# Out-projection squares in a PSUM bank, and the tail of chunk 0 ordered ahead of chunk 1

## The chip, the cores and the metric

One NeuronCore of a Trainium2 chip runs the whole kernel. The metric is device time in microseconds (us) from the start of the program to its end. Matmuls run on TensorE (PE), elementwise work on VectorE (DVE), ScalarE (ACT) and GpSimd (POOL), and SyncE (SP) issues the DMAs. SBUF is the on-chip memory of 128 partitions; PSUM has 8 banks of 512 float32 per partition, into which TensorE accumulates.

## What is computed

One inference step of one decoder layer: 1024 prompt tokens and 8 x 4 sample tokens, 1056 together, with 1024 channels. Everything is float32. The part around the change is `_finish`:

```python
mix = jnp.concatenate([attn_o.reshape(b, t, D_ATTN).astype(x.dtype), conv_o], axis=-1)
h = x + mix @ w_out
hn = rms_norm(h, norm_ffn_g)
return h + (jax.nn.silu(hn @ w_gate) * (hn @ w_up)) @ w_down

def rms_norm(x, g):
    xf = x.astype(jnp.float32)
    y = xf * lax.rsqrt(jnp.mean(xf * xf, axis=-1, keepdims=True) + RMS_EPS)
    return (y * g.astype(jnp.float32)).astype(x.dtype)
```

`w_out` is 1024 x 1024; the feed-forward width is 2816. Ahead of this stand a first norm, the input projection, three-branch attention and a short convolution; a final norm follows.

## The kernel before

Channels lie on partitions, tokens on the free axis. The 1056 tokens are cut into three chunks c = 0, 1, 2 of 352 columns, and 1024 channels into 8 tiles k or n of 128. A product is made in three passes from high and low parts (`three_pass`): both operands are split into a rounded part (fp32r) and the rest. One job is one 128 x 352 output tile over 8 input tiles, so 24 matmuls. The weights come as units of 128 x 1024; GpSimd splits each unit into `w_hi` and `w_lo` (a cast, L396, and a subtraction, L398) in a ring of three slots, after a wait for the jobs that last read the slot. The units of the out-projection are OUT0 to OUT0+7, those of the feed-forward begin with FFN0; FFN0+3 has a slot of its own.

Every engine runs its own program in the written order and waits on semaphores. In the out-projection:

- TensorE runs 24 jobs j in the order `OUT_ORDER`: tiles 0 and 1 of every chunk, tiles 2 to 4 chunk by chunk within a tile, then tiles 5 to 7 of chunk 0 (j = 15 to 17), of chunk 1 (18 to 20) and of chunk 2 (21 to 23). Job j goes to bank j % 6.
- VectorE adds each product to the residual (`add_product`, L1503: "evacuation", counts `h_done`). ScalarE squares the result into one of six SBUF buffers (`square`, L1059, counts `h_sq`). VectorE adds the squares of a chunk up in `ssum` (`add_squares`, L1513, counts `h_ss`), always one job behind the evacuation.
- When a chunk is complete, TensorE multiplies `ssum` with a matrix of ones (`sum_of_squares`, L854), which adds over the partitions: behind job 18 for chunk 0, behind job 22 for chunk 1 (`SUMS_BEHIND = [18, 22]`), and behind the first gate tile for chunk 2.
- Then, per chunk: VectorE divides by 1024 and adds epsilon (`mean_square`, L1186), ScalarE takes the root (`take_root`, L936), VectorE the reciprocal (L1192). For each of 8 tiles VectorE multiplies residual, gain and reciprocal (L1193, counts `y_done`), ScalarE copies that to the high part (`normal_hi`, L931, counts `hi_done`), VectorE subtracts for the low part (L1201, counts `lo_done`).
- The first feed-forward group follows in the order `FIRST_JOBS`: for each chunk c the tiles (0, c), (1, c) of the gate and (2, c), (3, c) of the up-projection (n, c). The gate tile (n, c) gets a silu on ScalarE (L1065) before the up tile (n + 2, c) may start, since they use the same bank. Tile (0, c) waits for all eight low parts of chunk c.

ScalarE needs a table load before a root and before a silu when the table in place is the other one; squares and copies work with either.

Of the kernel before, what the change touches and what calls it, by code (L numbers as in the profile page):

```python
# [28 lines left out]
P = 128  # L29
# [6 lines left out]
NC = 3  # L36
# [37 lines left out]
def build(nc, xT, w, gains, taps, conv_state, state_k, state_v, yT, kT, v_out, conv_tail):  # L74
    with ExitStack() as ctx:
# [305 lines left out]
        def _(pool):  # L381
# [104 lines left out]
            for u in range(OUT0 + 3, FFN0 + 16):  # L486
                straight(u)
                hidden_low(0, u)
# [21 lines left out]
        def _(pe):  # L510
# [11 lines left out]
            def tile_job(bank, c, slot):  # L522
                for k in range(KT):
                    mm = three_pass(ps[:, bank, 0:CH], slot, k, slice(P * k, P * k + P),
                                    act_hi[:, k, cols(c)], act_lo[:, k, cols(c)], k == 0, k == KT - 1)
                mm.then_inc(job_done, 1)
# [183 lines left out]
            def out_job(j):  # L710

                n, c = OUT_ORDER[j]
                unit_ready(OUT0 + n)
                if j < 2:
                    pe.wait_ge(biased, 2 * STEPS)
                if j >= 6:
                    pe.wait_ge(h_done, j - 5)
                if j == 2:
                    pe.wait_ge(act_copied, copied_through(STEPS, 0))
                    pe.wait_ge(dve_copied, copied_through(STEPS - 1, 1))  # L720
                for i, k in enumerate((4, 5, 6, 7, 0, 1, 2, 3)):
# [3 lines left out]
                    mm = three_pass(ps[:, j % 6, 0:CH], (OUT0 + n) % RING, k, slice(P * k, P * k + P),  # L725
                                    hi[:, k % 4, cols(c)], lo[:, k % 4, cols(c)], i == 0, i == KT - 1)
                mm.then_inc(job_done, 1)
# [134 lines left out]
            def gate_up(it, g, first=False):  # L862
                if first:
                    for i, (n, c) in enumerate(FIRST_JOBS):
                        if n == 0:
                            pe.wait_ge(lo_done, KT * (c + 1))
                        if n >= 2:
                            pe.wait_ge(silu_done, FIRST_GATES.index((n - 2, c)) + 1)
                        unit_ready(FFN0 + n)
                        tile_job(3 * (n % 2) + c, c, None if n == 3 else (FFN0 + n) % RING)  # L870
                        if i == 0:
                            sum_of_squares(2)
                    return
# [55 lines left out]
        def _(act):  # L929
# [124 lines left out]
            def square(which, j):  # L1054
                n, c = H_ORDERS[which][j]
                act.wait_ge(h_done, NC * KT * which + j + 1)
                if j >= 6:
                    act.wait_ge((h_ss, last_ss)[which], j - 5)
                act.activation(sq6[j % 6], res[:, n, cols(c)], ACT.Square).then_inc(h_sq, 1)  # L1059
# [68 lines left out]
        def _(dve):  # L1128
# [59 lines left out]
            def normal(which, c, k, dst):  # L1188

                if k == 0:  # L1190
                    dve.wait_ge(root, NC * which + c + 1)
                    chain(dve.reciprocal(rstd[:, cols(c)], rstd[:, cols(c)]))  # L1192
                dve.scalar_tensor_tensor(dst, res[:, k, cols(c)], g_sb[:, which, k:k + 1], rstd[:, cols(c)],  # L1193
                                         ALU.mult, ALU.mult).then_inc(y_done, 1)

            def norm(which, c):
# [7 lines left out]
                for k in range(KT):  # L1204
# [3 lines left out]
                    normal(which, c, k, norm_slot(i))  # L1208
                    if k >= 1:
                        low(i - 1)  # L1210
                low(KT * c + KT - 1)
# [284 lines left out]
            def add_product(which, j):  # L1496
# [5 lines left out]
                bank = j % 6 if which == 0 else last_bank(j)  # L1502
# [3 lines left out]
            def add_squares(j):  # L1506
                n, c = OUT_ORDER[j]
                dve.wait_ge(h_sq, j + 1)
                if n == 0:
                    dve.tensor_copy(ssum[:, cols(c)], sq6[j % 6]).then_inc(h_ss, 1)  # L1510
# [12 lines left out]
            add_squares(NC * KT - 1)  # L1523
            norm(1, 1)
            mean_square(1, 2)
            norm(1, 2)
# [106 lines left out]
BIAS_BEHIND = [6, 7, 11, 12, 19, 20]  # L1633
SUMS_BEHIND = [18, 22]
# [6 lines left out]
def last_bank(i):  # L1641

    return 3 + i % LAST_RING
# [170 lines left out]
```

## Time and profile before

| | us |
|---|---|
| median of 3 runs | 1327.34 (1326.81 to 1327.90) |
| profiled execution, whole time | 1328.08 |
| its span | 1326.3 |
| TensorE busy | 1305.3, 98% of the span |
| VectorE busy | 477.5, 36% |
| ScalarE busy | 239.5, 18% |
| GpSimd busy | 502.1, 38% |

The span is the time between the first and the last recorded instruction. The out-projection lies from about 450 to 552 us of it; the changed part, the last six jobs and the norm between the out-projection and the first feed-forward group, from about 523 to 582 us. Lines such as L1513 are lines of the kernel before. A matmul's recorded length (0.32 us) is longer than the distance to the next, since matmuls overlap in the array.

### The profile page before, as it was taken

The page shows a single profiled execution, that of the slowest core. Times are in us where ns is not written, and L with a number is a line of the kernel's source. Part 1 is how long each engine was busy: PE and PEld are TensorE (multiplying, and loading weights), DVE is VectorE, ACT ScalarE, POOL GpSimd, SP SyncE. Part 2 cuts the span into 40 slices and gives each one's busy share as a digit, 9 for nine tenths or more (in the row PEclk, how much of TensorE's full clock was granted, in tenths as well). Part 3 has the DMA queues.
Part 4 walks back from the last instruction along what each step waited for, and adds up shares of the span by engine and source line. Part 5 has one row for each costly group of instructions (what it writes and reads, how often), then busy time and mean ns, then how long its engine had stood idle before and what let it go on. Part 6 is the DMA issues. An engine that isn't in the chain of part 4 may idle for free.

```text
span 1326.3 us, 20841 instructions
## 1 busy us (share of the span) xinstructions
PE 1305.3 (98%) x8512; PEld 1226.0 (92%) x8512; DVE 477.5 (36%) x886; ACT 239.5 (18%) x506; POOL 502.1 (38%) x475
## 2 busy tenths in 40 slices
PE   7999999999999999999999999999999999999997
PEld 7999987989666799899999999999999999999997
DVE  7844222444665333850313121221213130303046
ACT  6000110000777411331000000101010101010113
POOL 4432142222654232415343343434343333444335
PEclk9999999999999999999999999999999999999999
DMA  5534566252120221202111111111111111111103
GB/s 196 215 123 174 178 238 223 77 193 80 51 98 30 101 79 32 65 1 76 36 49 48 48 48 48 48 48 48 36 44 48 48 48 48 43 53 33 56 9 133
DMA packets 38084, 107.84 MB, mean 81 GB/s; under 512 B 4016, under 2 KB 16496, under 8 KB 36208
## 3 DMA queue, kind: packets, MB, share of 16 engines
q1 hardware_dynamic: 38000, 106.60, 23.4%
q8 instruction: 67, 1.10, 0.4%
q14 instruction: 17, 0.14, 0.0%
HBM read 95.73 MB, written 10.85 MB: 80 GB/s over the span
## 4 chain that ended last, share of the span: by engine, by line
PE 91%; DVE 4%; ACT 1%; issue 1%; DMA 1%; POOL 1%; SPq 0%; DVEq 0%; POOLq 0%
PE ps L518 20%; PE ps L519 19%; PE ps L520 19%; PE ps L907 6%; PE ps L909 6%; PE ps L908 6%; PE ps L660 3%; PE ps L705 2%; PE ps L684 2%; PE ps L637 1%; PE ps L638 1%; PE ps L639 1%; PE ps L609 1%; PE ps L581 1%; DVE out L1193 1%
## 5 line engine op out<-in xcount | busy, mean ns | idle before, releaser
L518 PE MATMUL ps<-act_hi,w_hi 128*128 128x352 f32 x1608 | 523.1, 325 | 8.6 <-DVE act_lo L1216 8.3
L519 PE MATMUL ps<-act_lo,w_hi 128*128 128x352 f32 x1608 | 516.5, 321 | 0.0
L520 PE MATMUL ps<-act_hi,w_lo 128*128 128x352 f32 x1608 | 516.2, 321 | 0.0
L518 PEld LDWEIGHTS ps<-act_hi,w_hi 128*128 128x128 f32 x1608 | 302.6, 188 | 23.0 <-issue 22.1
L519 PEld LDWEIGHTS ps<-act_lo,w_hi 128*128 128x128 f32 x1608 | 303.1, 188 | 0.2
L520 PEld LDWEIGHTS ps<-act_hi,w_lo 128*128 128x128 f32 x1608 | 302.2, 188 | 0.0
L394 POOL TENSOR_TENSOR gate_cell<-ones 128x1 f32<-128x1 f32 x92 | 18.0, 196 | 677.0 <-PE ps L520 462.6
L398 POOL TENSOR_TENSOR w_lo<-w_stage,w_hi 128x1024 fp32r<-128x1024 f32 x93 | 228.7, 2459 | 7.5
L1534 DVE TENSOR_TENSOR work<-ps,work 128x352 f32<-128x352 f32 x66 | 34.4, 524 | 443.6 <-PE ps L520 443.6
L1544 DVE TENSOR_TENSOR resid<-ps,resid 128x352 f32<-128x352 f32 x240 | 126.0, 525 | 102.7 <-PE ps L909 102.7
L907 PE MATMUL ps<-pair_hi,w_hi 128*128 128x352 f32 x504 | 162.8, 323 | 0.0
L908 PE MATMUL ps<-pair_lo,w_hi 128*128 128x352 f32 x504 | 162.3, 322 | 0.0
L909 PE MATMUL ps<-pair_hi,w_lo 128*128 128x352 f32 x504 | 162.2, 322 | 0.0
L396 POOL CAST w_hi<-w_stage 128x1024 fp32r<-128x1024 f32 x93 | 96.9, 1042 | 13.6 <-DVE work L1224 13.6
L1094 ACT ACTIVATE work<-ps 128x352 f32<-128x352 f32 x60 | 27.9, 464 | 401.4 <-PE ps L520 401.4
L909 PEld LDWEIGHTS ps<-pair_hi,w_lo 128*128 128x128 f32 x504 | 94.9, 188 | 0.0
L908 PEld LDWEIGHTS ps<-pair_lo,w_hi 128*128 128x128 f32 x504 | 94.8, 188 | 0.0
L907 PEld LDWEIGHTS ps<-pair_hi,w_hi 128*128 128x128 f32 x504 | 94.7, 188 | 0.0
L931 ACT ACTIVATE pair_hi<-work 128x352 fp32r<-128x352 f32 (+1 forms) x70 | 36.9, 531 | 286.5 <-DVE work L1534 211.2
L450 POOL TENSOR_SCALAR q_blk<-ident,row_rec 128x128 f32<-128x128 f32 x64 | 43.4, 690 | 71.9 <-DVE row_rec L1408 60.5
L482 POOL TENSOR_TENSOR pair_lo<-work,pair_hi 128x352 fp32r<-128x352 f32 x66 | 60.6, 946 | 0.0
L1503 DVE TENSOR_TENSOR resid<-ps,resid 128x352 f32<-128x352 f32 x48 | 25.0, 523 | 56.7 <-PE ps L520 48.0
(228 smaller groups left out, 1328.6 us busy)
## 6 DMA issues: line engine op xcount, KB each, us to landing
w_stage<-in_w SPq DMA_DIRECT2D x97, 512.0 KB, 3.5
resid<-in_state_k SPq DMA_DIRECT2D x8, 1792.0 KB, 8.0
v_buf<-in_state_v SPq DMA_DIRECT2D x14, 1024.0 KB, 5.4
resid<-in_xT SPq DMA_DIRECT2D x16, 528.0 KB, 7.0
out_yT<-resid SPq DMA_DIRECT2D x24, 176.0 KB, 1.8
q_d<-out SPq DMA_DIRECT2D x12, 176.0 KB, 5.0
out_kT<-out SPq DMA_DIRECT2D x12, 176.0 KB, 1.8
out_v<-out SPq DMA_DIRECT2D x16, 128.0 KB, 2.0
```

The costliest lines, as they stand in the source:

```text
L396: pool.tensor_copy(hi, w_stage[:, stage, :]).then_inc(w_split, 1)
L398: pool.tensor_tensor(lo, w_stage[:, stage, :], f32(hi), ALU.subtract).then_inc(w_split, 1)
L450: pool.tensor_scalar(recip[t % 4][h], ident[:, :], row_rec[:, x:x + 1], None, ALU.mult).then_inc(spread, 1)
L482: pool.tensor_tensor(pair_lo[:, 2 * (g % 2) + f, cols(c)], silu[:, f, cols(c)], f32(pair_hi[:, 2 * (g % 2) + f, cols(c)]), ALU.subtract).t ...
L518: pe.matmul(out, hi, rhs_hi, start=first, stop=False)
L519: pe.matmul(out, hi, rhs_lo, start=False, stop=False)
L520: return pe.matmul(out, lo, rhs_hi, start=False, stop=last)
L660: mm = pe.matmul(ps[:, 2 * h + half, 0:width], st_q[g % 2][r, P * i:P * i + P], st_k[g % 2][r, 512 * x:512 * x + width], start=True, stop= ...
L907: pe.matmul(out, hi, x_hi, start=(f == 0), stop=False)
L908: pe.matmul(out, hi, x_lo, start=False, stop=False)
L909: mm = pe.matmul(out, lo, x_hi, start=False, stop=(f == 1))
L1544: dve.tensor_tensor(res[:, n, cols(c)], ps[:, 6 + i % 2, 0:CH], res[:, n, cols(c)], ALU.add).then_inc(added, 1)
```

## The change

The squares no longer go to six SBUF buffers but to one PSUM bank, number 5 (`OUT_BANKS = 5`); the jobs get five banks instead of six. `add_squares(j)` stands right behind `add_product(j)`. The end is ordered by hand: VectorE does evacuations 19 to 22 and the additions of squares 19 to 21 between the tiles of chunk 0's norm, then the mean of chunk 1, addition 22, the reciprocal of chunk 1, evacuation and addition 23, and only then the norm of chunk 1 and that of chunk 2. ScalarE follows that order; the silus of the first group stand elsewhere. The first tile of a chunk waits for each low part as it comes to it, and GpSimd starts unit FFN0+1 only when chunk 0's low parts are done. The function `norm` is now `inverse_root` and `normals(c, ks)`, with the same instructions in them.

```diff
@@ gpsimd
             for u in range(OUT0 + 3, FFN0 + 16):
+                if u == FFN0 + 1:
+                    pool.wait_ge(lo_done, KT)
                 straight(u)
@@ tensor
-            def tile_job(bank, c, slot):
+            def tile_job(bank, c, slot, lows=None):
                 for k in range(KT):
+                    if lows is not None:
+                        pe.wait_ge(lo_done, lows + k + 1)
...
-                if j >= 6:
-                    pe.wait_ge(h_done, j - 5)
+                if j >= OUT_BANKS:
+                    pe.wait_ge(h_done, j - OUT_BANKS + 1)
...
-                        if n == 0:
-                            pe.wait_ge(lo_done, KT * (c + 1))
...
-                        tile_job(3 * (n % 2) + c, c, None if n == 3 else (FFN0 + n) % RING)
+                        tile_job(3 * (n % 2) + c, c, None if n == 3 else (FFN0 + n) % RING, KT * c if n == 0 else None)
@@ scalar
-                if j >= 6:
-                    act.wait_ge((h_ss, last_ss)[which], j - 5)
-                act.activation(sq6[j % 6], res[:, n, cols(c)], ACT.Square).then_inc(h_sq, 1)
+                if which == 0 and j >= 1:
+                    act.wait_ge(h_ss, j)
...
+                act.activation(sq6[j % 6] if which else ps[:, OUT_BANKS, 0:CH], res[:, n, cols(c)], ACT.Square
+                               ).then_inc(h_sq, 1)
...
-            for j in range(NC * KT):
+            for j in range(SUMS_BEHIND[0] + 1):
                 square(0, j)
-                if j in SUMS_BEHIND:
-                    take_root(1, SUMS_BEHIND.index(j))
-                if j == SUMS_BEHIND[0]:
-                    normal_hi(0)
-            next(first_silus)
+            take_root(1, 0)
+            normal_hi(0, range(0, 2))
+            square(0, 19)
+            normal_hi(0, range(2, 5))
+            square(0, 20)
+            normal_hi(0, range(5, 6))
+            square(0, 21)
+            normal_hi(0, range(6, 8))
+            take_root(1, 1)
+            square(0, 22)
+            square(0, 23)
             normal_hi(1, range(0, 2))
             next(first_silus)
-            normal_hi(1, range(2, 8))
+            normal_hi(1, range(2, 4))
+            next(first_silus)
+            normal_hi(1, range(4, 8))
             take_root(1, 2)
-            normal_hi(2, range(0, 3))
-            next(first_silus)
-            normal_hi(2, range(3, 6))
-            next(first_silus)
-            normal_hi(2, range(6, 8))
+            normal_hi(2, range(0, 8))
@@ vector
-                    dve.tensor_tensor(ssum[:, cols(c)], ssum[:, cols(c)], sq6[j % 6], ALU.add).then_inc(h_ss, 1)
+                    dve.tensor_tensor(ssum[:, cols(c)], ps[:, OUT_BANKS, 0:CH], ssum[:, cols(c)], ALU.add).then_inc(h_ss, 1)
 
-            for j in range(NC * KT):
+            for j in range(SUMS_BEHIND[0] + 1):
                 add_product(0, j)
-                if j >= 1:
-                    add_squares(j - 1)
-                if j in SUMS_BEHIND:
-                    mean_square(1, SUMS_BEHIND.index(j))
-                if j == SUMS_BEHIND[0]:
-                    norm(1, 0)
-            add_squares(NC * KT - 1)
-            norm(1, 1)
+                add_squares(j)
+            mean_square(1, 0)
+            inverse_root(0)
+            normals(0, range(0, 2))
+            add_product(0, 19)
+            normals(0, range(2, 3))
+            add_squares(19)
+            normals(0, range(3, 5))
+            add_product(0, 20)
+            normals(0, range(5, 6))
+            add_squares(20)
+            add_product(0, 21)
+            normals(0, range(6, 7))
+            add_squares(21)
+            normals(0, range(7, 8))
+            add_product(0, 22)
+            mean_square(1, 1)
+            add_squares(22)
+            inverse_root(1)
+            add_product(0, 23)
+            add_squares(23)
+            normals(1, range(0, 8))
             mean_square(1, 2)
-            norm(1, 2)
+            inverse_root(2)
+            normals(2, range(0, 8))
```

How the rows stand on the engines, at three places. First VectorE behind the mean of chunk 0, before (L1503 evacuation, L1513 addition of squares, L1186 mean, L1193 and L1201 the norm's multiply and subtraction):

```order
L1503 TENSOR_TENSOR resid<-ps,resid 128x352
L1513 TENSOR_TENSOR work<-work 128x352
L1186 TENSOR_SCALAR work<-ps 128x352
L1192 RECIPROCAL work<-work 128x352
L1193 SCALAR_TENSOR_TENSOR out<-resid,g_sb,work 128x352 x2
L1201 TENSOR_TENSOR act_lo<-out,act_hi 128x352
L1193 SCALAR_TENSOR_TENSOR out<-resid,g_sb,work 128x352
L1201 TENSOR_TENSOR act_lo<-out,act_hi 128x352
```

and in the changed kernel, where the line numbers are L1514, L1524, L1198, L1203, L1217 and L1210:

```order
L1514 TENSOR_TENSOR resid<-ps,resid 128x352
L1524 TENSOR_TENSOR work<-ps,work 128x352
L1198 TENSOR_SCALAR work<-ps 128x352
L1203 RECIPROCAL work<-work 128x352
L1217 SCALAR_TENSOR_TENSOR out<-resid,g_sb,work 128x352 x2
L1210 TENSOR_TENSOR act_lo<-out,act_hi 128x352
L1514 TENSOR_TENSOR resid<-ps,resid 128x352
L1217 SCALAR_TENSOR_TENSOR out<-resid,g_sb,work 128x352
L1210 TENSOR_TENSOR act_lo<-out,act_hi 128x352
L1524 TENSOR_TENSOR work<-ps,work 128x352
```

The additions read `ps`, and evacuation 19 and addition 19 moved from behind chunk 0's norm to between its tiles. Second, VectorE between the norms of chunks 0 and 1, before:

```order
L1201 TENSOR_TENSOR act_lo<-out,act_hi 128x352 x2
L1503 TENSOR_TENSOR resid<-ps,resid 128x352
L1513 TENSOR_TENSOR work<-work 128x352
L1186 TENSOR_SCALAR work<-ps 128x352
L1503 TENSOR_TENSOR resid<-ps,resid 128x352
L1513 TENSOR_TENSOR work<-work 128x352 x2
L1192 RECIPROCAL work<-work 128x352
```

(the pair L1503, L1513 stands there four times) and in the changed kernel:

```order
L1210 TENSOR_TENSOR act_lo<-out,act_hi 128x352 x2
L1514 TENSOR_TENSOR resid<-ps,resid 128x352
L1198 TENSOR_SCALAR work<-ps 128x352
L1524 TENSOR_TENSOR work<-ps,work 128x352
L1203 RECIPROCAL work<-work 128x352
L1514 TENSOR_TENSOR resid<-ps,resid 128x352
L1524 TENSOR_TENSOR work<-ps,work 128x352
L1217 SCALAR_TENSOR_TENSOR out<-resid,g_sb,work 128x352 x2
```

Only evacuations 22 and 23 are left there, and the reciprocal of chunk 1 moved ahead of the last of them. Third, ScalarE from the first silu of the feed-forward on (L1065 silu, L931 high parts, L936 root), before:

```order
L1065 ACT_TABLE_LOAD
L1065 ACTIVATE work<-ps 128x352
L931 ACTIVATE act_hi<-out 128x352 x2
L1065 ACTIVATE work<-ps 128x352
L931 ACTIVATE act_hi<-out 128x352 x6
L936 ACT_TABLE_LOAD
L936 ACTIVATE work<-work 128x352
L931 ACTIVATE act_hi<-out 128x352 x3
L1065 ACT_TABLE_LOAD
L1065 ACTIVATE work<-ps 128x352
L931 ACTIVATE act_hi<-out 128x352 x3
L1065 ACTIVATE work<-ps 128x352
```

and in the changed kernel (L1073, L933, L938):

```order
L933 ACTIVATE act_hi<-out 128x352 x2
L1073 ACT_TABLE_LOAD
L1073 ACTIVATE work<-ps 128x352
L933 ACTIVATE act_hi<-out 128x352 x2
L1073 ACTIVATE work<-ps 128x352
L933 ACTIVATE act_hi<-out 128x352 x4
L938 ACT_TABLE_LOAD
L938 ACTIVATE work<-work 128x352
L933 ACTIVATE act_hi<-out 128x352 x8
L1073 ACT_TABLE_LOAD
L1073 ACTIVATE work<-ps 128x352 x4
```

The first silu moved behind the first two high parts of chunk 1, and the third, that of gate tile (0, 1), from behind three high parts of chunk 2 to behind all eight.

## Rows read from the trace of the kernel before

**Rows 1.** The page: the span, and each engine's busy time, share and instructions.
```profile
span 1326.3 us, 20841 instructions
PE 1305.3 (98%) x8512; PEld 1226.0 (92%) x8512; DVE 477.5 (36%) x886; ACT 239.5 (18%) x506; POOL 502.1 (38%) x475
```

**Rows 2.** TensorE's waits from 525 to 580 us: in total, times, longest.
```profile
PE ps L854 <- DVE work L1513: 3.9, 3, 2.3
PE ps L518 <- ACT work L1065: 0.3, 1, 0.3
```

**Rows 3.** Timeline, TensorE: start, length, line, operation, [idle before <-releaser].
```profile
526.68 0.32 PE L520 MATMUL ps<-act_hi,w_lo 128*128 128x352 f32 x1
528.05 0.86 PE L854 MATMUL ps<-work,ones 128*128 128x352 f32 x2 [1.05 <-DVE work L1513]
528.91 0.32 PE L519 MATMUL ps<-pair_lo,w_hi 128*128 128x352 f32 x1
...
546.46 0.86 PE L854 MATMUL ps<-work,ones 128*128 128x352 f32 x2 [2.29 <-DVE work L1513]
549.25 0.50 PE L520 MATMUL ps<-pair_hi,w_lo 128*128 128x352 f32 x1
549.55 0.50 PE L518 MATMUL ps<-pair_hi,w_hi 128*128 128x352 f32 x1
...
577.29 0.43 PE L518 MATMUL ps<-act_hi,w_hi 128*128 128x352 f32 x1 [0.26 <-ACT work L1065]
```

**Rows 4.** Windows of TensorE: length, busy, granted clock, DMA share, GB/s.
```profile
544.00:548.00 4.00, 1.71 (x8) 0.93 0.37 131
548.00:552.00 4.00, 4.00 (x18) 0.64 0.42 135
```

**Rows 5.** Timeline, VectorE: two evacuations, one job apart.
```profile
523.22 0.53 DVE L1503 TENSOR_TENSOR resid<-ps,resid 128x352 f32<-128x352 f32 x1 [2.86 <-PE ps L520]
...
527.04 0.53 DVE L1503 TENSOR_TENSOR resid<-ps,resid 128x352 f32<-128x352 f32 x1 [2.86 <-PE ps L520]
```

**Rows 6.** Timeline, VectorE: additions of squares (L1513), norm (L1193), evacuations, reciprocal.
```profile
527.48 0.52 DVE L1513 TENSOR_TENSOR work<-work 128x352 f32<-128x352 f32 x1
532.42 1.08 DVE L1193 SCALAR_TENSOR_TENSOR out<-resid,g_sb,work 128x352 f32<-128x352 f32 x2
...
541.00 0.52 DVE L1503 TENSOR_TENSOR resid<-ps,resid 128x352 f32<-128x352 f32 x1
542.29 0.51 DVE L1503 TENSOR_TENSOR resid<-ps,resid 128x352 f32<-128x352 f32 x1
542.72 2.28 DVE L1513 TENSOR_TENSOR work<-work 128x352 f32<-128x352 f32 x1
...
553.19 3.86 DVE L1513 TENSOR_TENSOR work<-work 128x352 f32<-128x352 f32 x2
556.97 2.34 DVE L1192 RECIPROCAL work<-work 128x352 f32<-128x352 f32 x1
559.34 1.97 DVE L1193 SCALAR_TENSOR_TENSOR out<-resid,g_sb,work 128x352 f32<-128x352 f32 x2
```

**Rows 7.** Timeline, GpSimd: weight splits.
```profile
540.50 0.19 POOL L394 TENSOR_TENSOR gate_cell<-ones 128x1 f32<-128x1 f32 x1 [24.80 <-PE ps L520]
542.06 2.55 POOL L398 TENSOR_TENSOR w_lo<-w_stage,w_hi 128x1024 fp32r<-128x1024 f32 x1
...
552.99 1.04 POOL L396 CAST w_hi<-w_stage 128x1024 fp32r<-128x1024 f32 x1
558.02 2.40 POOL L398 TENSOR_TENSOR pt_lo<-w_stage,pt_hi 128x1024 fp32r<-128x1024 f32 x1
```

**Rows 8.** Timeline, ScalarE: a square, then a table load and silu.
```profile
527.60 0.50 ACT L1059 ACTIVATE work<-resid 128x352 f32<-128x352 f32 x1 [3.32 <-DVE resid L1503]
...
575.48 1.28 ACT L1065 ACT_TABLE_LOAD   x1
576.78 0.46 ACT L1065 ACTIVATE work<-ps 128x352 f32<-128x352 f32 x1
```

More of the change, by code:

```diff
@@ L724, in out_job @@
                         pe.wait_ge(mix_lo, STEPS // 2 - 2 + c)
-                    mm = three_pass(ps[:, j % 6, 0:CH], (OUT0 + n) % RING, k, slice(P * k, P * k + P),
+                    mm = three_pass(ps[:, j % OUT_BANKS, 0:CH], (OUT0 + n) % RING, k, slice(P * k, P * k + P),
                                     hi[:, k % 4, cols(c)], lo[:, k % 4, cols(c)], i == 0, i == KT - 1)
@@ L1056, in square @@
                 act.wait_ge(h_done, NC * KT * which + j + 1)
-                if j >= 6:
-                    act.wait_ge((h_ss, last_ss)[which], j - 5)
-                act.activation(sq6[j % 6], res[:, n, cols(c)], ACT.Square).then_inc(h_sq, 1)
+                if which == 0 and j >= 1:
+                    act.wait_ge(h_ss, j)
+                if which == 0 and j == 0:
+                    act.wait_ge(act_copied, copied_through(STEPS, 0))
+                    act.wait_ge(dve_copied, copied_through(STEPS - 1, 1))
+                if which == 1 and j >= 6:
+                    act.wait_ge(last_ss, j - 5)
+                act.activation(sq6[j % 6] if which else ps[:, OUT_BANKS, 0:CH], res[:, n, cols(c)], ACT.Square
+                               ).then_inc(h_sq, 1)
             def first_silu():
@@ L1186, in mean_square, with inverse_root, normals @@
                 dve.tensor_scalar((rstd if which else r_in)[:, cols(c)], ps[:, bank, 0:CH], 1.0 / D, EPS, ALU.mult, ALU.add).then_inc(mean_sq, 1)
[L1188 to L1196, printed above, removed]
+            def inverse_root(c):
+                dve.wait_ge(root, NC + c + 1)
+                chain(dve.reciprocal(rstd[:, cols(c)], rstd[:, cols(c)]))
+            def normals(c, ks):
                 def low(i):
@@ L1202, in low @@
                                       ALU.subtract).then_inc(lo_done, 1)
-                for k in range(KT):
+                for k in ks:
                     i = KT * c + k
@@ L1207, in norm @@
                         dve.wait_ge(lo_done, i - 1)
-                    normal(which, c, k, norm_slot(i))
+                    dve.scalar_tensor_tensor(norm_slot(i), res[:, k, cols(c)], g_sb[:, 1, k:k + 1], rstd[:, cols(c)],
+                                             ALU.mult, ALU.mult).then_inc(y_done, 1)
                     if k >= 1:
                         low(i - 1)
-                low(KT * c + KT - 1)
+                    if k == KT - 1:
+                        low(i)
             def raw_low(k):
@@ L1501, in add_product @@
                     dve.wait_ge(x2_in[n], 16)
-                bank = j % 6 if which == 0 else last_bank(j)
+                bank = j % OUT_BANKS if which == 0 else last_bank(j)
                 dve.tensor_tensor(res[:, n, cols(c)], ps[:, bank, 0:CH], res[:, n, cols(c)],
@@ L1509, in add_squares @@
                 if n == 0:
-                    dve.tensor_copy(ssum[:, cols(c)], sq6[j % 6]).then_inc(h_ss, 1)
+                    dve.tensor_copy(ssum[:, cols(c)], ps[:, OUT_BANKS, 0:CH]).then_inc(h_ss, 1)
                 else:
                     dve.wait_ge(h_ss, OUT_ORDER.index((n - 1, c)) + 1)
-                    dve.tensor_tensor(ssum[:, cols(c)], ssum[:, cols(c)], sq6[j % 6], ALU.add).then_inc(h_ss, 1)
-            for j in range(NC * KT):
+                    dve.tensor_tensor(ssum[:, cols(c)], ps[:, OUT_BANKS, 0:CH], ssum[:, cols(c)], ALU.add).then_inc(h_ss, 1)
+            for j in range(SUMS_BEHIND[0] + 1):
                 add_product(0, j)
-                if j >= 1:
-                    add_squares(j - 1)
-                if j in SUMS_BEHIND:
-                    mean_square(1, SUMS_BEHIND.index(j))
-                if j == SUMS_BEHIND[0]:
-                    norm(1, 0)
-            add_squares(NC * KT - 1)
-            norm(1, 1)
+                add_squares(j)
[20 more added lines that the diff above has]
+            normals(1, range(0, 8))
             mean_square(1, 2)
-            norm(1, 2)
+            inverse_root(2)
+            normals(2, range(0, 8))
             def hidden_of(it, g, first=False):
@@ L1633 @@
 BIAS_BEHIND = [6, 7, 11, 12, 19, 20]
+OUT_BANKS = 5
 SUMS_BEHIND = [18, 22]
```

## Prediction

> **What bounds the kernel now.** I read the page first: TensorE is busy 98% of the span [rows 1], so the time is TensorE's work plus the few gaps in it, and a change on the other engines can only touch gaps. The list of waits for the stretch 525 to 580 us shows all the gaps that this part has [rows 2]: TensorE waits three times at the ones-matmul of L854 (`sum_of_squares`), 3.9 us together, and once, 0.3 us, for a silu. The timeline of TensorE places them [rows 3]: 1.05 us before the sum of chunk 0 (528.05), 2.29 us before that of chunk 1 (546.46), so 0.55 us of the 3.9 before that of chunk 2, and 0.26 us before the third gate-and-up tile of chunk 1 (577.29), which needs the silu of (0, 1). Behind the second gap the granted clock falls: the two windows of [rows 4] lack 0.07 x 4 + 0.36 x 4 = 1.72 us of clock, that is 3.44 us at 1.2 GHz in place of 2.4. A matmul is then issued every 0.29 us (549.25 to 549.55 in [rows 3]) and not every 0.159 (24 of them in 3.82 us, the distance of two evacuations in [rows 5]). So 3.44 us give back only 3.44 x 0.159 / 0.293 = 1.87: 1.57 us are lost. Gaps and clock together are 4.15 + 1.57 = 5.7 us, the most that the stretch holds.
>
> Why are the sums late? VectorE's rows tell it [rows 6]. An addition of squares (L1513, two operands in SBUF) takes 0.52 us alone (527.48), but 2.28 us at 542.72, and the two at 553.19 take 3.86. GpSimd was in a weight split each time: its subtraction of 542.06 ends at 544.61, and the addition ends 0.4 us later, at 545.00 [rows 7]. The multiplies of L1193 (also two in SBUF) show it at 559.34: 1.97 us for two that take 1.08 at 532.42, while GpSimd's subtraction ran from 558.02 to 560.42 [rows 7]. Evacuations (L1503, PSUM and SBUF) and the reciprocal (one operand) are not stretched: 0.51 us at 542.29 and 2.34 us at 556.97, beside the same subtractions. So VectorE's instructions with two SBUF operands and GpSimd's exclude each other, for a whole instruction, and others run on.
>
> **The change, part by part.** *Additions read PSUM.* 21 of the 24 additions and 3 copies change their source. Nearest row: an evacuation, 0.53 us, also PSUM and SBUF. Most lie in VectorE's idle time between jobs, so they cost nothing; if a square written to PSUM took 0.7 us instead of its 0.50 [rows 8], product, square and addition would still take 1.8 of the 3.82 us that a job lasts. The five banks in place of six ask for an evacuation one job earlier, which is four jobs old: nothing. With one bank for the squares, a square waits for the addition before it, and the high parts wait behind it on ScalarE; in the new order that addition always stands ahead of the evacuation that the square needs, so this wait is never the last.
>
> *Sum of chunk 0.* Job 17's tile is evacuated at 523.22; its square and addition are now done by 523.22 + 0.53 + 0.50 + 0.52 and some 0.1 of signals, 524.9, before job 18 ends at 527.0. Gap 1 goes, 1.05 us, and with the pipeline's refill 1.21 (528.05 less 526.84).
>
> *The interleaved tail, VectorE.* I walk its new order. Evacuation 18 at 527.04, square, addition, mean: 529.1; the root stands behind its table load as now (square to 528.1, load 1.28, root 0.50), and the reciprocal runs from 529.9 to 532.2. Chunk 0's normals: eight multiplies and eight subtractions last from 532.42 to the evacuation at 541.00, 8.6 us. Three evacuations and three additions at 0.44 apart are pushed in: 2.6, of which some 0.5 fills waits for ScalarE. GpSimd begins the split of unit FFN0 at 539.3, when job 21 ends (540.50 less the 1.21): the seventh multiply meets its cast (+0.4) and the sixth subtraction its subtraction of 2.4 (+2.2). Chunk 0 ends at 532.2 + 8.6 + 2.1 + 2.7 = 545.6. The addition of square 20 lies ahead of that collision, near 539.5, so the sum of chunk 1 is ready when TensorE arrives: 526.84 + 0.70 for a sum + 4 x 3.82 = 542.8. **Gap 2 and the fall of the clock behind it go.** Job 23 ends near 547.5. (The new wait of a first tile for each low part only loosens one that [rows 2] do not show.)
>
> Then evacuation 22, mean, root, square and addition: 548.0; the second reciprocal 2.35: 550.3; evacuation 23, square, addition (0.53 + 0.50 + 0.52 and signals): 551.9. TensorE wants the last sum after the first gate tile, at 542.8 + 0.70 + 3.82 + 3.82 = 551.15, so **gap 3 is about 0.85, not 0.55.**
>
> *GpSimd's new wait.* Unit FFN0+1 waits for chunk 0's eighth low part, 545.6 (TensorE releases it at 543.0). Queued behind it are units +1, +2, +3, each 0.13 + 1.04 + 0.15 + 2.4 = 3.7 us [rows 7] and some holds by VectorE: they run on end to 557.3. TensorE needs unit +1 at 552.7, +2 at 556.5; they are done at 549.5 and 553.2. So the wait costs TensorE nothing, but the splits now cover the start of chunk 1's normals: the first multiply at 551.86 is held 1.2 us, the second 0.9, the first subtraction 2.1 (it waits for the subtraction that ends at 557.3). Now only 0.9 is lost there.
>
> *The silus.* Chunk 1's normals: 551.9 + 8.6 + 4.2 = 564.7; mean 565.2, root behind its table load, reciprocal 565.9 to 568.3; the last multiply of chunk 2 ends at 568.3 + 7.6 = 575.9 and the last high part (0.50) at 576.4. Only then does ScalarE reach the table load of 1.28 us and the silu of 0.46 [rows 8]: 578.1. Before, that silu stood between the third and the fourth high part of chunk 2 and was done at 577.24 (576.78 + 0.46). TensorE wants it sooner than before: last sum at 552.0 (+0.70), gate tile (1, 0) to 556.5; a wait of 0.8 for the first silu, which now stands behind two high parts and a table load (557.26); four tiles of 3.82: 572.6. So **a new wait of about 5.5 us** stands before tile (2, 1), which starts at 578.1 where it now starts at 577.3: **0.85 us later**, and all that the first two gaps gave is spent there.
>
> *The clock at the new wait.* [rows 4] show a fall behind 2.29 us of waiting, and none behind 1.05 (the matmul at 528.91 has its usual 0.32 us, [rows 3]). Behind 5.5 us I take one fall of the same price, 1.57 us; below it is 0 (as behind 1.05), above it twice that, 3.1, since the wait is 2.4 times the 2.29. After 578 everything on TensorE follows in the same order with no gap from this part, so the shift stays to the end.
>
> The Trainium skill ("ScalarE: Activation LUTs", What ACT_TABLE_LOAD costs) counts a drain of about 1.38 us with each switch, some 2.66 us in all. Here the silu starts 1.30 us after its load begins, so the row decides; by the page the wait would be 1.4 us longer and the time 1331.2.
>
> **Sum.** 0.85 + 1.57 = 2.4 us on the profiled execution's 1328.08 us (span 1326.3 and 1.8 around it). That execution lies 0.74 above the median, inside what one fall of the clock is worth; I move the median by the same 2.4: 1327.34 + 2.4 = **1329.8 us**. Can be told from no change: about 0.2%, 2.7 us.
>
> **Rivals.** (1) *The forecast*: gaps 1 and 2 traded for the silu wait; 1328.4 to 1331.3. It straddles the bound: 56%, of which 31 below +0.2% and 25 above. (2) *The holds are lighter.* The chain of VectorE has 6.9 us of holds in it (0.4, 2.2, 1.2, 0.9, 2.1), each a matter of which engine asks first. With half of them the wait is near 2 us and the tile starts at 574.7; without a fall of the clock that is 1327.3 - 2.6 = 1324.7 (with one 1326.3), and without any holds up to 5.6 us are won, 1321.7. For it: the splits need not meet those instructions. Against: chunk 1's normals run for 8.6 us and three splits in a row for 11.7. 20%, 18 of them below -0.2%. (3) *The wait as forecast, but no clock lost*: 1327.34 + 0.85 = 1328.2; 10%. (4) *Slower, by the clock*: after the long wait the clock comes back only after twice the 3.44 us; 3.1 + 0.85 = 3.95, 1331.3 or more. It decides for slower once the clock loses over 1.8 us, that is over 4 us at the lower level behind 578. Speaks for it: a wait over twice as long; against: the one fall seen came back at once. 14%.
>
> **How the numbers follow.** Faster is case 2's 18%. Same: 31 + 10 + 2 = 43%. Slower: 25 + 14 = 39%. The low end is case 2 with six tenths of the holds gone (4.2 us, the tile at 573.9 and so 3.4 earlier than now), 1324.0; the high end case 4 with a little more, 1331.8. That leaves some 2 in 10 out.
>
> **What would show it.** In the changed profile: no wait before the first two sums; no addition of squares over 0.6 us; a wait of 0.5 to 1 us at the last sum and at (2, 0); GpSimd's splits of three units end to end from about 546 to 557; ScalarE's silu of (0, 1) behind all 24 high parts at about 577.6; TensorE idle 5 to 6 us before it, and a granted clock under 1 behind that. The prediction is wrong if chunk 2's last high part is done before 574, if (2, 1) starts before 576, or if the clock does not fall, or for longer than 4 us.

## The result, and the profile after

| | median us | range | runs |
|---|---|---|---|
| before | 1327.26 | 1326.56 to 1328.63 | 10 |
| changed | 1330.52 | 1329.84 to 1330.83 | 10 |

The ratio is 1.0021, with a 95% interval of 1.0013 to 1.0029: 0.2% slower, 3.3 us between the medians. The forecast was 1329.8. The interval does not hold 1, so the slowdown is real, if small. The profiled execution of the changed kernel took 1329.98 us, its span is 1328.2.

TensorE's waits from 515 to 590 us (in total, times, longest), which answer to [rows 2]. The three waits for a sum, 3.9 us, are one of 0.6, and the wait for a silu of 0.3 us is two, 5.5 together:

```profile
PE ps L520 <- ACT work L1073: 5.5, 2, 5.1
PE ps L858 <- DVE work L1524: 0.6, 1, 0.6
```

TensorE's timeline in the same profile, for [rows 3]. The sums of chunks 0 and 1 have no wait left. TensorE still waits at the last sum (551.92), for the first silu (556.99) and for the silu of (0, 1) (577.86); behind 577.86 a matmul is issued every 0.29 us, until 581.4:

```profile
527.13 0.75 PE L858 MATMUL ps<-work,ones 128*128 128x352 f32 x2
...
551.92 0.86 PE L858 MATMUL ps<-work,ones 128*128 128x352 f32 x2 [0.56 <-DVE work L1524]
...
556.99 0.43 PE L520 MATMUL ps<-act_hi,w_hi 128*128 128x352 f32 x1 [0.39 <-ACT work L1073]
...
577.86 0.62 PE L520 MATMUL ps<-act_hi,w_hi 128*128 128x352 f32 x1 [5.12 <-ACT work L1073]
578.29 0.49 PE L521 MATMUL ps<-act_lo,w_hi 128*128 128x352 f32 x1
...
581.44 0.32 PE L520 MATMUL ps<-act_hi,w_hi 128*128 128x352 f32 x1
```

The windows of TensorE (length, busy, granted clock, DMA share, GB/s), for [rows 4]: the clock is full where it fell before, and falls some 31 us later. Here it lacks (0.26 + 0.17) x 4 = 1.72 us, that is 3.44 us at the lower level of 1.2 GHz, as long as in the profile of before:

```profile
544.00:548.00 4.00, 4.00 (x27) 1.00 0.39 135
...
576.00:580.00 4.00, 2.14 (x7) 0.74 0.00 0
580.00:584.00 4.00, 4.00 (x23) 0.83 0.00 0
```

VectorE's timeline, for [rows 6]. L1524 is the addition of squares, L1217 and L1210 the norm's multiply and subtraction:

```profile
540.20 0.82 DVE L1217 SCALAR_TENSOR_TENSOR out<-resid,g_sb,work 128x352 f32<-128x352 f32 x1
540.94 2.72 DVE L1210 TENSOR_TENSOR act_lo<-out,act_hi 128x352 fp32r<-128x352 f32 x1
543.59 0.51 DVE L1524 TENSOR_TENSOR work<-ps,work 128x352 f32<-128x352 f32 x1
...
551.35 0.52 DVE L1524 TENSOR_TENSOR work<-ps,work 128x352 f32<-128x352 f32 x1 [0.53 <-ACT ps L1066]
551.79 2.84 DVE L1217 SCALAR_TENSOR_TENSOR out<-resid,g_sb,work 128x352 f32<-128x352 f32 x2
554.56 2.71 DVE L1210 TENSOR_TENSOR act_lo<-out,act_hi 128x352 fp32r<-128x352 f32 x1
```

and GpSimd's, for [rows 7]:

```profile
540.73 2.56 POOL L398 TENSOR_TENSOR w_lo<-w_stage,w_hi 128x1024 fp32r<-128x1024 f32 x1
545.76 0.19 POOL L394 TENSOR_TENSOR gate_cell<-ones 128x1 f32<-128x1 f32 x1 [2.48 <-DVE act_lo L1210]
...
550.61 2.36 POOL L398 TENSOR_TENSOR w_lo<-w_stage,w_hi 128x1024 fp32r<-128x1024 f32 x1
553.03 1.22 POOL L396 CAST pt_hi<-w_stage 128x1024 fp32r<-128x1024 f32 x1
554.33 2.55 POOL L398 TENSOR_TENSOR pt_lo<-w_stage,pt_hi 128x1024 fp32r<-128x1024 f32 x1
```

Read the two together. The additions take 0.51 to 0.53 us wherever GpSimd is. Each stretched instruction ends 0.4 us behind a GpSimd instruction: the subtraction of 540.94 at 543.66 (GpSimd's at 543.29), the two multiplies at 554.63 (the cast at 554.25), the subtraction of 554.56 at 557.27 (GpSimd's at 556.88). A hold is the time that a stretched instruction takes beyond its usual one; they are 0.24 (the multiply of 540.20, against 0.58) + 2.20 + 1.76 + 2.19 = 6.4 us.

ScalarE's timeline, for [rows 8]. A square into PSUM takes 0.47 us, not more than one into SBUF. The last high part of chunk 2 ends at 576.04; only then come the table load and, at 577.35, the third and fourth silu:

```profile
527.89 0.47 ACT L1066 ACTIVATE ps<-resid 128x352 f32<-128x352 f32 x1 [3.35 <-DVE resid L1514]
...
575.54 0.50 ACT L933 ACTIVATE act_hi<-out 128x352 fp32r<-128x352 f32 x1 [0.56 <-DVE out L1217]
576.05 1.28 ACT L1073 ACT_TABLE_LOAD   x1
577.35 0.82 ACT L1073 ACTIVATE work<-ps 128x352 f32<-128x352 f32 x2
```

### The profile page after: what moved, and what is told of

Same layout as the page of the kernel before. It is cut to its first block, busy times and chain, and to the rows that moved or that the text cites. A ratio compares the mean times of both kernels' runs of the same rounds, so it can differ in the third digit from the quotient of the medians.

```text
span 1328.2 us, 20847 instructions
## 1 busy us (share of the span) xinstructions
PE 1305.2 (98%) x8512; PEld 1226.2 (92%) x8512; DVE 474.5 (36%) x886; ACT 238.9 (18%) x506; POOL 500.4 (38%) x475
## 4 chain that ended last, share of the span: by engine, by line
PE 91%; DVE 5%; ACT 2%; issue 1%; DMA 1%; POOL 1%; SPq 0%; DVEq 0%; POOLq 0%
PE ps L520 20%; PE ps L521 19%; PE ps L522 19%; PE ps L909 6%; PE ps L910 6%; PE ps L911 6%; PE ps L664 3%; PE ps L709 2%; PE ps L688 2%; PE ps L641 1%; PE ps L642 1%; PE ps L643 1%; DVE out L1217 1%; PE ps L613 1%; PE ps L585 1%
## 5 line engine op out<-in xcount | busy, mean ns | idle before, releaser
L1570 DVE TENSOR_TENSOR resid<-ps,resid 128x352 f32<-128x352 f32 x240 | 126.1, 525 | 102.7 <-PE ps L911 102.7
L933 ACT ACTIVATE pair_hi<-work 128x352 fp32r<-128x352 f32 (+1 forms) x70 | 36.9, 532 | 286.4 <-DVE work L1560 211.1
L1018 ACT ACTIVATE resid<-resid,row_neg 128x384 f32<-128x384 f32 (+5 forms) x48 | 42.1, 881 | 0.4
```

What stands on the lines that cost most here:

```text
L1018: act.activation(prow(t, h), prow(t, h), ACT.Exp, scale=-1.0, bias=row_neg[:, x:x + 1], accum_out=row_sum[:, x:x + 1]).then_inc(exped, 1)
L1570: dve.tensor_tensor(res[:, n, cols(c)], ps[:, 6 + i % 2, 0:CH], res[:, n, cols(c)], ALU.add).then_inc(added, 1)
```

## The experiments

Each time is a median; the runs of before that were taken beside them had medians of 1326.85 (e1 to e4), 1327.04 (e5 to e8) and 1327.94 us (e9). Ratios are to those. Where the text compares an experiment with the changed kernel, it subtracts medians that were taken at different times, and the runs of before beside them differ by up to 0.4 us (1326.85 to 1327.26), so such a difference is uncertain by about as much.

### e1: the changed kernel, two silus put back

```diff
             take_root(1, 2)
-            normal_hi(2, range(0, 8))
+            normal_hi(2, range(0, 3))
+            next(first_silus)
+            normal_hi(2, range(3, 6))
+            next(first_silus)
+            normal_hi(2, range(6, 8))
```

> The changed kernel, with only the third and fourth silu put back between the high parts of chunk 2 (behind 3 and behind 6 of them). My theory (the order of the silus makes the 5.1 us wait at tile (2, 1)): the silu of (0, 1) comes right behind the third high part and a table load, the wait at (2, 1) falls to 0.3 us or less, the clock keeps its level, and 5.1 + 1.6 us come back: about 1323.9. Rival (the wait is VectorE's late norm, the silus only show it): at most 1.5 us come back, 1329 or more.

Measured: 1323.08 us (1322.90 to 1323.28), ratio 0.9966 [0.9954, 0.9978]. TensorE's waits of its profile:

```profile
PE ps L858 <- DVE work L1528: 0.6, 1, 0.6
PE ps L520 <- ACT work L1073: 0.4, 1, 0.4
```

The wait at (2, 1) is gone, and the clock is full in every window from 524 to 592 us. ScalarE's timeline shows the table load behind the third high part and the silu at 572.01:

```profile
570.72 1.28 ACT L1073 ACT_TABLE_LOAD   x1
572.01 0.47 ACT L1073 ACTIVATE work<-ps 128x352 f32<-128x352 f32 x1
```

Two instructions moved, and 7.4 us came back (7.0 if each kernel is taken against its own runs of before). The rival (VectorE's late norm alone) falls: the last high part of chunk 2 ended at 576.69 here, no earlier than in the changed kernel (576.04).

### e2: the kernel before, with the silus late

```diff
             take_root(1, 2)
-            normal_hi(2, range(0, 3))
-            next(first_silus)
-            normal_hi(2, range(3, 6))
-            next(first_silus)
-            normal_hi(2, range(6, 8))
+            normal_hi(2, range(0, 8))
```

> The kernel before, with only the third and fourth silu moved behind all eight high parts of chunk 2. My theory: tile (2, 1) waits for the table load and silu behind chunk 2's last high part, which ended at 581.45: 1.3 + 0.5 us later, so it starts at 583.2 where it started at 577.3, 5.9 us later, and the clock falls a second time for 1.6 us: about 1334.8. Rival (the silu's place matters only in the changed kernel's order): 1327.3 to 1329.

Measured: 1334.63 us (1334.01 to 1335.61), ratio 1.0055 [1.0041, 1.0069], 7.8 us over before. TensorE's waits, and two of its windows:

```profile
PE ps L518 <- ACT work L1065: 5.5, 1, 5.5
PE ps L854 <- DVE work L1509: 3.8, 3, 2.3
```
```profile
580.00:584.00 4.00, 2.62 (x9) 0.55 0.00 0
584.00:588.00 4.00, 4.00 (x18) 0.59 0.00 0
```

The late silus alone cost either order the same: 7.4 us in the changed one, 7.8 here. In this execution the clock was low for (0.45 + 0.41) x 4 / 0.5 = 6.9 us, twice as long as in the changed kernel's profile. The forecast of 1334.8 was met by two errors that cancel: chunk 2's last high part ended at 579.56 and not at 581.45, since no silu stands between the high parts any more, so the tile started at 581.38 and not at 583.2; and the clock cost more than the 1.6 us assumed.

### e3: the changed kernel, TensorE kept busy in the wait

```diff
+                        if (n, c) == (2, 1):
+                            for _ in range(7):
+                                pe.matmul(ps[:, 7, 0:CH], ones[:, :], ssum[:, 0:CH], start=True, stop=True)
                         if n >= 2:
                             pe.wait_ge(silu_done, FIRST_GATES.index((n - 2, c)) + 1)
```

> The changed kernel, with seven 128x352 float32 matmuls of ones and ssum into the idle bank 7 ahead of tile (2, 1), whose result nobody reads: 7 x 0.70 us fill 4.9 of the 5.1 us that TensorE waits there. My theory (the fall of the clock behind the wait costs 1.6 us): the granted clock stays at 1.00 behind 578, and 1.6 us come back, about 1328.9. Rival (the clock costs nothing there, or falls anyway): 1330.5 or a little more.

Measured: 1328.36 us (1328.09 to 1328.84), ratio 1.0009 [1.0000, 1.0018]. Tile (2, 1) starts at 577.71, as late as in the changed kernel, with this wait left behind the added matmuls:

```profile
577.71 0.43 PE L520 MATMUL ps<-act_hi,w_hi 128*128 128x352 f32 x1 [0.98 <-ACT work L1076]
```
```profile
576.00:580.00 4.00, 3.02 (x17) 1.00 0.00 0
580.00:584.00 4.00, 4.00 (x27) 1.00 0.00 0
```

The clock stays full, and 2.2 us come back although tile (2, 1) starts no earlier. Against each kernel's own runs of before it is 1.8 us, and between the profiled spans 1.7 (1328.2 less 1326.5). So the fall of the clock costs the changed kernel 1.7 to 2.2 us; 1.6 was forecast.

### e4: an order with no wait

```diff
             square(0, 23)
-            normal_hi(1, range(0, 2))
             next(first_silus)
-            normal_hi(1, range(2, 4))
+            normal_hi(1, range(0, 2))
             next(first_silus)
-            normal_hi(1, range(4, 8))
+            normal_hi(1, range(2, 8))
             take_root(1, 2)
-            normal_hi(2, range(0, 8))
+            next(first_silus)
+            normal_hi(2, range(0, 4))
+            next(first_silus)
+            normal_hi(2, range(4, 8))
...
             add_squares(22)
-            inverse_root(1)
             add_product(0, 23)
             add_squares(23)
+            inverse_root(1)
```

> The changed kernel in another order: first silu ahead of chunk 1's high parts, second behind two of them, third ahead of chunk 2's high parts (its table load beside VectorE's reciprocal), fourth behind four of them; and evacuation and addition 23 ahead of the reciprocal of chunk 1. My theory, by the same walk: none of the three waits is left (0.6, 0.4 and 5.1 us) and the clock does not fall: 6.1 + 1.6 = 7.7 us less than the changed kernel, about 1322.8. Rival (VectorE's chain, held by the splits, is the limit): no better than the kernel with the silus put back, 1324 or more, with a wait at (2, 1) or (0, 2).

Measured: 1321.24 us (1321.20 to 1321.65), ratio 0.9954 [0.9940, 0.9967]. It beats both kernels: 5.6 us under before, 9.3 under the changed one. TensorE's windows of this profile from 524 to 600 us have no gap at all (length, busy, granted clock):

```profile
524.00:550.00 26.00, 26.00 (x162) 1.00 0.07 22
550.00:576.00 26.00, 26.00 (x164) 1.00 0.18 61
576.00:600.00 24.00, 24.00 (x153) 1.00 0.13 44
```

The rival's limit of 1324 is passed: VectorE's chain, holds and all, is fast enough once the silus do not queue behind it. This run moves four silus and evacuation 23 at once, so it doesn't say what each is worth.

### e5: the kernel before, squares in PSUM only

```diff
-                if j >= 6:
-                    pe.wait_ge(h_done, j - 5)
+                if j >= OUT_BANKS:
+                    pe.wait_ge(h_done, j - OUT_BANKS + 1)
...
-                act.activation(sq6[j % 6], res[:, n, cols(c)], ACT.Square).then_inc(h_sq, 1)
+                act.activation(sq6[j % 6] if which else ps[:, OUT_BANKS, 0:CH], res[:, n, cols(c)], ACT.Square
+                               ).then_inc(h_sq, 1)
...
-                    dve.tensor_tensor(ssum[:, cols(c)], ssum[:, cols(c)], sq6[j % 6], ALU.add).then_inc(h_ss, 1)
+                    dve.tensor_tensor(ssum[:, cols(c)], ps[:, OUT_BANKS, 0:CH], ssum[:, cols(c)], ALU.add).then_inc(h_ss, 1)
```

> The kernel before, with only the squares in PSUM bank 5 and the jobs in five banks; every engine's order is that of before, an addition still stands one evacuation late. My theory (GpSimd's splits hold the additions with two SBUF operands, and one PSUM operand frees them): no addition over 0.6 us, gap 1 stays at 1.05 us, gap 2 falls from 2.3 to 1.2 us or less, too short for a fall of the clock, gap 3 goes: 2.2 us of waits and 1.6 us of clock, about 1323.1. Rival (the order, not the operand, made the sums late): 1326 or more.

Measured: 1324.69 us (1323.98 to 1324.89), ratio 0.9979 [0.9970, 0.9988]: 2.35 us less than before, 1.6 less than forecast. TensorE's waits, and an addition that runs beside GpSimd's cast of 545.03:

```profile
PE ps L854 <- DVE work L1519: 2.3, 2, 1.2
```
```profile
545.26 0.53 DVE L1519 TENSOR_TENSOR work<-ps,work 128x352 f32<-128x352 f32 x1 [0.16 <-ACT ps L1064]
```

Gap 1 stays at 1.05 us, gap 2 is 1.20 with the clock full behind it, gap 3 is gone, as the theory had it. So the operand alone makes the sums come 1.6 us earlier in all, and the rival falls; why the median moved less than the walk said is taken up below.

### e6: the changed kernel, squares in SBUF again

```diff
-                act.activation(sq6[j % 6] if which else ps[:, OUT_BANKS, 0:CH], res[:, n, cols(c)], ACT.Square
+                act.activation(sq6[j % 6], res[:, n, cols(c)], ACT.Square
...
-                    dve.tensor_tensor(ssum[:, cols(c)], ps[:, OUT_BANKS, 0:CH], ssum[:, cols(c)], ALU.add).then_inc(h_ss, 1)
+                    dve.tensor_tensor(ssum[:, cols(c)], ssum[:, cols(c)], sq6[j % 6], ALU.add).then_inc(h_ss, 1)
```

> The changed kernel, with the squares and their additions in the SBUF buffers again; orders, five job banks and waits as changed. My theory: addition 22 is held by the split of unit FFN0+1 and addition 23 by that of FFN0+2, 2 us each or less; the sum of chunk 2 is waited for 2.5 to 3 us, chunk 2's last high part ends 1.5 us later: 1332.0 (the longer wait at the sum lies ahead of the wait at (2, 1) and costs nothing of its own). Rival (the operand is worth nothing): 1330.5.

Measured: 1332.85 us (1332.05 to 1333.09), ratio 1.0038 [1.0024, 1.0052], 2.3 us over the changed kernel. TensorE's waits, and VectorE's addition 22 and chunk 1's first multiplies:

```profile
PE ps L520 <- ACT work L1073: 3.8, 1, 3.8
PE ps L858 <- DVE work L1524: 2.6, 1, 2.6
```
```profile
547.72 2.28 DVE L1524 TENSOR_TENSOR work<-work 128x352 f32<-128x352 f32 x1 [0.95 <-ACT work L1066]
...
553.82 3.97 DVE L1217 SCALAR_TENSOR_TENSOR out<-resid,g_sb,work 128x352 f32<-128x352 f32 x2
```

Only addition 22 is held, by 1.8 us; addition 23 happens to fall free. The last high part of chunk 2 ends at 577.71, 1.7 us later than in the changed kernel (1.5 forecast), so the rival (the operand is worth nothing) falls. The clock falls behind the 2.65 us at the sum, for 3.4 us, and again at (2, 1), for 6.8 us; the forecast had counted neither the first fall nor the longer second one.

### e7: the changed kernel without GpSimd's new wait

```diff
-                if u == FFN0 + 1:
-                    pool.wait_ge(lo_done, KT)
```

> The changed kernel without GpSimd's new wait for chunk 0's low parts ahead of unit FFN0+1. My theory: that split now meets the last three tiles of chunk 0's norm (2.5 us later), and the splits of +2 and +3 end by 555.3, so that chunk 1's norm is held less; chunk 2's last high part comes 0.4 us earlier, the wait at the last sum is 3.4 us and that at (2, 1) 3.4: 1330.1, no difference. Rival (the new wait pushes the splits onto chunk 1's norm and so makes the loss): 1328.5 or less. Second rival (it shields chunk 0's norm, which decides): 1332 or more.

Measured: 1331.01 us (1329.97 to 1332.91), ratio 1.0026 [1.0016, 1.0035]: not distinguishable from the changed kernel's 1.0021. TensorE's waits, and VectorE where the split of FFN0+1 now meets chunk 0's norm:

```profile
PE ps L856 <- DVE work L1522: 3.0, 1, 3.0
PE ps L518 <- ACT work L1071: 2.6, 1, 2.6
```
```profile
544.85 1.05 DVE L1215 SCALAR_TENSOR_TENSOR out<-resid,g_sb,work 128x352 f32<-128x352 f32 x1
545.82 3.15 DVE L1208 TENSOR_TENSOR act_lo<-out,act_hi 128x352 fp32r<-128x352 f32 x2
...
563.65 0.53 DVE L1208 TENSOR_TENSOR act_lo<-out,act_hi 128x352 fp32r<-128x352 f32 x1 [1.95 <-ACT act_hi L931]
```

Most of the holds moved from chunk 1's norm to chunk 0's, and both rivals (1328.5 or less, 1332 or more) fall. The last row was in no forecast: VectorE waits 1.95 us for a high part that stands on ScalarE behind the second silu, and that silu waits 2.9 us for gate tile (1, 0), late by TensorE's own wait and low clock. In this order TensorE and VectorE can hold each other up through ScalarE.

### e8: the changed kernel with two short splits

```diff
-                pool.tensor_tensor(lo, w_stage[:, stage, :], f32(hi), ALU.subtract).then_inc(w_split, 1)
+                pool.tensor_tensor(lo[:, 0:n], w_stage[:, stage, 0:n], f32(hi)[:, 0:n], ALU.subtract).then_inc(w_split, 1)
...
+                      n=8 if u in (FFN0 + 1, FFN0 + 2) else 1024)
```

> The changed kernel, but GpSimd's subtraction for the weight units FFN0+1 and FFN0+2 takes 8 of 1024 columns; the low parts of these two weight tiles are left stale, so the output is not the reference's. My theory (the splits hold chunk 1's norm for 4 us): the two splits end before it begins, only that of FFN0+3 still meets it, about 2.3 us of holds go, and the wait at (2, 1) falls from 5.1 to 3 us: about 1328.4. Rival (the holds lie beside other waits of VectorE): 1330.5.

Measured: 1329.29 us (1328.94 to 1330.14), ratio 1.0012 [1.0003, 1.0021], 1.2 us under the changed kernel. TensorE's waits, and the shortened and the full subtraction on GpSimd:

```profile
PE ps L521 <- ACT work L1074: 4.6, 2, 3.9
PE ps L859 <- DVE work L1525: 0.6, 1, 0.6
```
```profile
549.03 0.20 POOL L398 TENSOR_TENSOR w_lo<-w_stage,w_hi 128x8 fp32r<-128x8 f32 x1
550.74 1.04 POOL L396 CAST pt_hi<-w_stage 128x1024 fp32r<-128x1024 f32 x1 [1.50 <-DMA w_stage<-in_w]
551.85 2.38 POOL L398 TENSOR_TENSOR pt_lo<-w_stage,pt_hi 128x1024 fp32r<-128x1024 f32 x1
```

The holds do lie on the path, but less of them went than forecast: the wait at (2, 1) fell by 1.3 us, not by 2. The split of FFN0+3 had to wait 1.5 us for its weights, which are loaded into the stage that FFN0+1 frees, and so still met the first two multiplies.

### e9: the kernel before, TensorE kept busy before the sum of chunk 1

```diff
+                if c == 1:
+                    for _ in range(3):
+                        pe.matmul(ps[:, 7, 0:CH], ones[:, :], ssum[:, 0:CH], start=True, stop=True)
                 pe.wait_ge(h_ss, chunk_end(c))
```

> The kernel before, with three 128x352 float32 matmuls of ones and ssum into bank 7 ahead of the sum of chunk 1, whose result nobody reads: 3 x 0.70 us fill 2.1 of the 2.29 us that TensorE waits there. It asks how much of the shift from before to after is clock: the profiled execution of before lost 1.6 us to it behind this wait, that of the changed kernel 1.7, the medians moved by 3.3 us and the profiled spans by 1.9. My theory (before loses clock here in only some of its executions, the changed kernel behind its 5.1 us in all of them): the granted clock stays at 1.00, the runs lie within 0.6 us of each other, and the median falls by less than the 1.6 us of its profile, by 0.5 to 1.2: about 1326.2. Rival (before loses the full 1.6 us in every execution): 1325.4 or less. Second rival (the fall costs nothing, since the silu of (0, 1) sets the start of tile (2, 1) either way): 1327.0.

Measured: 1326.98 us (1326.69 to 1327.44, 11 runs), ratio 0.9994 [0.9985, 1.0003]; before beside it 1327.94 (1326.32 to 1329.42, 15 runs). The wait at the sum is 0.49 us and the clock stays:

```profile
546.87 0.86 PE L857 MATMUL ps<-work,ones 128*128 128x352 f32 x2 [0.49 <-DVE work L1516]
```
```profile
544.00:548.00 4.00, 3.51 (x15) 1.00 0.39 129
```

The ratio's interval holds 1, so the medians alone don't say what the fall costs before. The single runs say more. The 67 runs of before in this case fall into two groups: 37 from 1326.13 to 1327.34 us, 30 from 1327.90 to 1329.42, none between. Where a run's mean granted clock is on record (57 of them), it is 0.998 or 0.999 in the lower group, and 0.997 (19 runs) or 0.998 (7) in the upper. The groups' medians, 1326.8 and 1328.3, lie 1.5 us apart, which is what the prediction read for one fall (1.57), and the profiled execution of before, with its fall, took 1328.08 and belongs to the upper one. All 11 runs of e9 stand where the lower group does (1326.69 to 1327.44), and spread over 0.75 us, where the 15 runs of before beside them spread over 3.1. So before pays for a fall of the clock in somewhat less than half of its executions, about 1.5 us each time, and e9 takes it away. That supports the theory and speaks against both rivals; the theory's number (1326.2) was off because the median of such a mixture jumps with the share of the two groups: it was 1326.85 beside e1 to e4 and 1327.94 here. No execution of the lower group was profiled, so that it is this fall which divides them is inferred.

## Why the prediction was right, point by point

**The bound, and the 5.7 us in the stretch.** Right in kind: e4 takes all waits out of the stretch and is 5.6 us under before. But 5.7 was too small for the execution that it was read from: between the profiled spans of before and e4 lie 6.8 us (1326.3 to 1319.5). A wait costs TensorE more than its idle time, 1.21 us for the first gap of 1.05 as the prediction noted for that gap alone, and the pair of matmuls of a sum takes 0.86 us behind a wait and 0.75 without (527.13). That the medians differ by just 5.6 is partly luck, since before's median holds little of its fall of the clock.

**Additions with one PSUM operand are not held.** Right: 0.51 to 0.53 us in the changed kernel beside GpSimd's work, 2.28 for addition 22 in e6. That squares written to PSUM would cost nothing was right too (0.47 us). The Trainium skill ("SBUF — State Buffer", SBUF: two separate sides) states the rule behind it: VectorE with two SBUF inputs and GpSimd take a shared port pair as an exclusive lock for a whole instruction. The stretched rows, each ending 0.4 us behind a GpSimd instruction, agree.

**Gaps 1 and 2 and the fall behind gap 2 go; gap 3 stays.** Right. Gap 3 is 0.56 us where 0.85 was forecast, the first silu's 0.39 where 0.8 was. Both sizes are off by 0.3 to 0.4 us; the walk added up a chain of small delays, and no run separates them.

**GpSimd's new wait costs TensorE nothing and moves the splits onto chunk 1's norm.** Right: three splits end to end from 545.8 to 556.9 (forecast 545.6 to 557.3), holds of 6.4 us (forecast 6.9). So rival 2, lighter holds, fell. e7 adds that without that wait as much is lost elsewhere, and e8 that 1.3 us of the wait at (2, 1) hang on two of the splits.

**The third silu behind all high parts.** Right, and the step on which all rests: wait 5.12 us (5.5), last high part 576.04 (576.4), tile (2, 1) at 577.86 (578.1). e1 shows it as the cause by two moved instructions, e2 by the same move in the kernel before. The drain of about 1.38 us that the Trainium skill ("ScalarE: Activation LUTs", What ACT_TABLE_LOAD costs) adds to a table load is not there: the silu stands 1.30 us behind the start of its load in this profile too.

**The clock at the new wait.** The mechanism was right, e3 shows it by itself, and rival 3 (no clock lost) fell; the size was right for the profile and perhaps low for the median. The profile lost what was forecast (12 matmuls from 577.86 to 581.44 in 3.58 us where 1.91 would do: 1.7), but the median holds up to 2.2 (1330.52 less 1328.36). e2 and e6 show how it can be more: their clocks stayed low for 6.8 to 6.9 us, of which 5.9 us, up to 587.3, lie behind the start of tile (2, 1) in e2. That would be the fourth rival in part. Four of the changed kernel's ten runs have a mean granted clock of 0.996, where the profiled one has 0.998, which fits; none of those four was profiled, so it is not shown.

**The sum.** Right within its range, but the median moved by 3.3 us and not by 2.4. The weak step is "I move the median by the same 2.4". The rows came from an execution of before's upper group, with the whole fall of the clock in it, while before's median lies at the edge of the lower group, where the fall isn't paid (e9). From the upper group's median, 1328.3, it is 2.2 us to the changed kernel's 1330.52, from the lower group's, 1326.8, it is 3.7. Had the 2.4 been added to the execution that was read, 1328.08, the sum would have been 1330.5. Some of that nearness is luck: between the two profiled spans lie only 1.9 us. Tile (2, 1) starts 0.57 us later, or 0.3 counted from the sum of chunk 0, which the changed profile reaches 0.29 later; 0.85 was forecast. The clock's 1.7 us makes the rest, and the profiled execution of the changed kernel lies 0.5 us under its median. The same wrong base explains most of what e5 fell short by, 1.6 us: its profiled span is 3.4 us under that of before (1326.3 to 1322.9), where the walk said 3.8.

**The range and the marks.** The result is the first case, 1328.4 to 1331.3, which was given 56%. The whole range, 1324.0 to 1331.8, held a faster kernel and a slower one alike, so that the time fell into it says little by itself. What bears the forecast out are the marks under "What would show it": all were met but one, the wait at (2, 0), which is 0.39 us and not 0.5 to 1. The five banks in place of six and the first tile's wait for each low part were not tested by themselves; no wait of TensorE in the changed profile falls on either.

## What to carry to other kernels

When an operand moves to free one engine, walk every engine's written order to the point where they meet again: here the operand was worth 2.4 us (e5) and the new order, with its silus put back, 1.6 more (e5 to e1), but two activations left at the end of a third engine's queue cost 7.4. A queue that waits in order is as late as the latest thing ahead in it, so an instruction that TensorE waits for belongs ahead of work that is paced by another engine, and its table load where that engine is busy anyway (in e4 beside VectorE's reciprocal). And look at the single runs before you take a base: where they fall into two groups, find out to which the profiled execution belongs, and add the change worked out from it to that group and not to the median of all.

## What the runs showed of the hardware that was not expected

The spread of a kernel's times follows the clock. Kernels in whose profile the clock keeps its level in this stretch lie within 0.4 to 0.9 us (e1: 0.4 in 6 runs; e4: 0.45 in 5; e3 and e9: 0.75 in 11 each; e5: 0.9 in 11). Before, whose waits are 2.3 us at most, spreads over 3.1 us in 15 runs, and e7, with waits of 3.0 and 2.6 us, over 2.9 in 10.

How long the clock stays low does not simply follow the wait. It was 3.4 us behind waits of 2.3 (before), 2.6 (e6 and e7), 3.9 (e8) and 5.1 us (the changed kernel), and 6.8 to 6.9 us behind 3.0 (e7), 3.8 (e6) and 5.5 us (e2). Nor does it fall each time: behind the 2.29 us in the profile of before it fell, behind nearly the same wait in e2's profile it did not (TensorE's row, and its window with the clock at 1.00):

```profile
546.83 0.86 PE L854 MATMUL ps<-work,ones 128*128 128x352 f32 x2 [2.26 <-DVE work L1509]
```
```profile
548.00:552.00 4.00, 4.00 (x27) 1.00 0.39 133
```

Behind waits of 1.05 and 1.20 us no profile shows a fall.
